# The projection of the per-layer input, moved from the first stage to the stretch before the last gate

## What is computed

```python
u = rms_norm(h, g_pre)
z = u @ w_in                       # 2048 x 22528, attention, retention, gates
...                                # attention, retention, merge of both
y = merged @ w_o
h = h + rms_norm(y, g_post)
h = h + sigmoid(h @ w_ple_gate) * (p @ w_ple_proj)
```

## Time and profile before

| | us |
|---|---|
| median of three runs | 3043.8 |
| the profiled execution | 3037.74 |
| its span | 3035.8 |
| PE busy | 2911.3 (96%) |
| DVE busy | 1772.7 (58%) |
| ACT busy | 1137.2 (37%) |
| granted PE clock over the span | 0.98 |

### The profile page before, as it was taken

One profiled execution on the slowest core, in us unless ns is written; L12 is line 12 of the kernel. 1 busy time (PEld: TensorE's weight loads), 2 busy tenths in 40 slices (PEclk: granted clock), 3 DMA queues, 4 the chain that ended last, 5 costly groups with the idle time before them and its releaser, 6 DMA issues.

```text
span 3035.8 us, 57013 instructions
## 1 busy us (share of the span) xinstructions
PE 2911.3 (96%) x23406; PEld 2856.8 (94%) x23406; DVE 1772.7 (58%) x3159; ACT 1137.2 (37%) x2078; POOL 362.2 (12%) x537
## 2 busy tenths in 40 slices
PE   6899999999999999999999999999999999997898
PEld 6899999999999998989999999999999999997897
DVE  5557666676566666576676676665654433424532
ACT  6344343444444433333333333434343222323222
POOL 2000000000001002112112112110001100001211
PEclk8999999999999999999999999999999999998899
DMA  8555656656566454456465456476657665554353
GB/s 254 160 168 176 205 170 201 193 184 193 168 190 194 161 194 158 140 192 210 153 212 188 157 199 215 158 256 213 246 198 290 214 234 191 205 187 147 116 186 110
DMA packets 380307, 575.64 MB, mean 190 GB/s; under 512 B 16456, under 2 KB 340872, under 8 KB 376840
## 3 DMA queue, kind: packets, MB, share of 16 engines
q1 hardware_dynamic: 336448, 428.32, 41.1%
q0 software_dynamic: 43600, 143.69, 15.6%
HBM read 515.67 MB, written 232.42 MB: 246 GB/s over the span
## 4 chain that ended last, share of the span: by engine, by line
PE 82%; DMA 5%; DVE 5%; DVEq 3%; ACT 2%; issue 1%; ACTq 1%; SPq 0%; POOL 0%; POOLq 0%
PE acc L524 52%; PE acc L536 21%; DMA raw_weights<-in_w_in 1%; PE aux L756 1%; PE aux L767 1%; DVEq L1704 1%; DVE weights L1287 1%; PE aux L777 1%; DVE stage_buffers L1873 1%; ACT weights L933 1%; DMA y_scr<-stage_buffers 1%; PE aux L649 1%; PE aux L833 1%; DVEq L1392 1%; DMA stage_buffers<-in_x_prompt 1%
## 5 line engine op out<-in xcount | busy, mean ns | idle before, releaser
L524 PE MATMUL acc<-moving,weights 128*128 128x260 f32 x12384 | 1574.5, 285 | 7.5 <-DVE sampled L1368 7.5
L524 PEld LDWEIGHTS acc<-moving,weights 128*128 128x128 f32 x12384 | 1516.8, 189 | 16.9 <-issue 8.3
L1287 DVE TENSOR_TENSOR weights<-raw_weights,weights 128x512 fp32r<-128x512 f32 (+1 forms) x1030 | 697.8, 686 | 707.5 <-ACT weights L933 660.0
L933 ACT ACTIVATE weights<-raw_weights 128x512 fp32r<-128x512 f32 (+1 forms) x1030 | 634.1, 625 | 1185.5 <-PE acc L524 438.7
L536 PE MATMUL acc<-moving,weights 128*128 128x260 f32 x5760 | 711.2, 286 | 48.8 <-DVE moving L1843 20.5
L536 PEld LDWEIGHTS acc<-moving,weights 128*128 128x128 f32 x5760 | 705.3, 191 | 52.2 <-DVE weights L1287 22.3
L524 PE MATMUL acc<-combined_moving,weights 128*128 128x260 f32 x3096 | 430.2, 289 | 3.2 <-DVE partial_sums L1401 2.4
L524 PEld LDWEIGHTS acc<-combined_moving,weights 128*128 128x128 f32 x3096 | 394.9, 191 | 8.9 <-issue 5.9
L1368 DVE SCALAR_TENSOR_TENSOR stage_buffers<-acc,partial_sums 128x260 f32<-128x260 f32 x344 | 146.5, 478 | 165.8 <-PE acc L524 165.7
L933 ACT ACTIVATE weights<-combined_weights 128x512 fp32r<-128x512 f32 x172 | 108.1, 629 | 295.8 <-PE acc L524 279.7
L1287 DVE TENSOR_TENSOR weights<-combined_weights,weights 128x512 fp32r<-128x512 f32 x172 | 118.5, 689 | 145.8 <-ACT weights L933 145.0
(11 more groups left out here) (256 smaller groups left out, 1783.8 us busy)
## 6 DMA issues: line engine op xcount, KB each, us to landing
out<-in_cache_win SPq DMA_DIRECT2D x128, 1023.5 KB, 8.8
raw_weights<-in_w_in SPq DMA_DIRECT2D x96, 1024.0 KB, 6.2
raw_weights<-in_w_in SPq DMA_DIRECT2D x160, 512.0 KB, 5.3
out<-in_cache_win SPq DMA_DIRECT2D x32, 1022.0 KB, 10.9
out<-stage_buffers POOLq DMA_DIRECT2D x120, 256.0 KB, 3.3
stage_buffers<-in_cache_win POOLq DMA_DIRECT2D x48, 512.0 KB, 5.5
stage_buffers<-in_state_ret POOLq DMA_DIRECT2D x64, 256.0 KB, 3.7
raw_weights<-in_w_r_out SPq DMA_DIRECT2D x16, 1024.0 KB, 7.3
```

The costliest lines, as they stand in the source:

```text
L524: mm = pe.matmul(acc[:, m, half, 0:HC], W[:, g % AHEAD, wp, kk, :], mov(up, kk), start=(start and kk == 0 and n == 0), stop=(stop and kk = ...
L933: act.activation(W[:, g % AHEAD, 0, 0:src.shape[1]], src, ACT.Copy).then_inc(s_whi, 1)
L1287: dve.tensor_tensor(W[:, g % AHEAD, 1, 0:src.shape[1]], src, W[:, g % AHEAD, 0, 0:src.shape[1]].bitcast(F32), ALU.subtract).then_inc(s_wre ...
```

## The change

The projection's 16 chunks are now a pair of their own, PL (mode P), between the w_o pairs and the gate pairs. p and its transposes move too: SP loads p at the first w_r pair, PE turns it within the third w_o pair. The split of p goes to a tile of its own (`turned`), and the 16 projected tiles stay on chip in memory that the seven-product pairs no longer use (`projected`). The DRAM scratch and its stores and loads are gone. In the first stage nothing but x is prepared; weights of pair 0 are loaded at once, and their first ten chunks are converted before or among the tiles of x. The first tiles prepared are now 8 to 15. In the stretch before the gate, ACT and DVE interleave the projection's conversions and copies with the tiles of h. For all pairs the half of `raw` whose chunk comes first is loaded first.

```diff
-       "F0": [("raw", c, m) for c in (1, 2, 3, 0) for m in range(2)],
-       "F1": [("raw", c, m) for c in (2, 3, 0, 1) for m in range(2)],
+       "F": [("raw", c, m) for c in (2, 3, 0, 1) for m in range(2)],
+       "P": [("two", n // 8, n % 8) for n in range(KD)],
...
     def halves_of(p):
-        return [half for half in (1, 0) if any(o[0] == "raw" and o[1] // 2 == half for o in OPS[p.mode])]
+        seen = [half_of(p.first + n) for n in range(p.n)]
+        return sorted({half for half in seen if half is not None}, key=seen.index)
...
-    FIRST_KS = [*range(4, KD), 2, 3, 0, 1]
+    FIRST_KS = [*range(8, KD), *range(8)]
...
+            if q == WR:
+                for slot in range(2):
+                    sp.wait_ge(s_rnewst[slot], 16 * QB * 2 * H)
+                sp.dma_start(p_nat, p_prompt[0, 0].rearrange("(t p) c -> p t c", p=P)).then_inc(s_xload[5], 16)
...
+            elif q == PL:
+                copies = 0
...
+        for q in range(WO, PL):
+            plain_pair(pairs[q], {0: [input_turns]} if q == WO + 2 else {}, ...)
+        pe.wait_ge(s_plo, 3)
+        for n in range(KD):
+            if n == 2:
+                square_means()
+            pe.wait_ge(s_wready, pairs[PL].first + n + 1)
+            acc_ready(n % 2)
+            ...  # 12 matmuls, as line 640 before
...
         for n in range(KD):
             act.wait_ge(s_u, count.due(s_u))
-            if n == KD - 2:
-                act.wait_ge(s_used, N_PLE)
             act.activation(U[:, 0, FIRST_KS[n], :], utmp[:, n % 4, :], ACT.Copy).then_inc(s_uhi, 1)
-            act.wait_ge(s_used, n + 1)
-            if n >= PPR:
-                act.wait_ge(s_ppst[n // 4 - 2], 16)
-            act.activation(halves(pp_out[:, n % PPR, :]), acc[:, n % 2, :, 0:HC], ACT.Copy).then_inc(...)
-            act.drain().then_inc(s_pp, 1)
-            hi(n + AHEAD)
+            if n in (9, 11, 13, 15):
+                hi(AHEAD + (n - 9) // 2)
...
+        for n in range(KD):
+            if n == 1:
+                norm_std()
+            projected_out(n)
+            hi(pairs[PL].first + n + AHEAD)
+            if n in (9, 11, 13, 15):
+                h_tile((n - 9) // 2)
+        for n in range(4, KD):
+            h_tile(n)
+            if n in (9, 11, 13, 15):
+                hi(pairs[WG].first + AHEAD + (n - 9) // 2)
...
+        g = pairs[PL].first + AHEAD
+        lo(g)
         dve.wait_ge(s_std, count.due(s_std))
         dve.reciprocal(nrs, nrs)
         dve.drain()
+        lo(g + 1)
         LAG = 3
         for n in range(KD + LAG):
             if n < KD:
+                normed_tile(n)
             if n >= LAG:
                 moving_lo(n - LAG, M)
+            if n < 7:
+                lo(g + 2 * n + 2)
+                lo(g + 2 * n + 3)
+            if n - LAG in (9, 11, 13, 15):
+                lo(pairs[WG].first + AHEAD + (n - LAG - 9) // 2)
```

More of the change, by code:

```diff
@@ L96 @@
 AHEAD = 6
-N_PLE = 16
 class Pair:
@@ L257, in build @@
     sg_in, tmp = t(2, TC), t(TC)
-    pp_in = t(2, TC)
+    p_rows = t(2 * TC)
+    p_nat, ps_nat = p_rows[:, 0:TB * PLE].rearrange("p (t c) -> p t c", t=TB), t(PLE)
+    pT = [turned[:, n] for n in range(2)]
+    projected = [*(projected_14[:, n, :] for n in range(14)), p_rows[:, 0:TC], p_rows[:, TC:2 * TC]]
     sqb, sqsum, nrs = sg_in, tmp, sg_in[:, 0, :]
@@ L888, in _, with input_turns @@
-        fills.add("norm", 0)
+        def input_turns():
+            pe.wait_ge(s_xload[5], count.due(s_xload[5], skip=1))
+            for j in range(2):
+                pe.wait_ge(s_free[2 + j], count.due(s_free[2 + j]))
+                for tb in range(TB):
+                    mm = pe.transpose(aux[:, 2 + j, tb * P:(tb + 1) * P], p_nat[:, tb, j * P:(j + 1) * P], ident[:])
+                mm.then_inc(s_full[2 + j], 1)
+                fills.add(f"p{j}", 2 + j)
+            pe.wait_ge(s_free[1], count.due(s_free[1]))
+            for j in range(2):
+                mm = pe.transpose(aux[:, 1, j * NS:(j + 1) * NS], ps_nat[0:NS, j * P:(j + 1) * P], ident[0:NS, 0:NS])
+            mm.then_inc(s_full[1], 1)
+            fills.add("ps", 1)
@@ new lines, in square_means @@
+        def square_means():
+            pe.wait_ge(s_sqsum, 1)
+            pe.wait_ge(s_free[0], count.due(s_free[0]))
+            pe.wait_ge(s_free[1], count.due(s_free[1]))
+            pe.matmul(aux[:, 0, 0:HC], mean_d[:], sqsum[:, 0:HC], start=True, stop=True)
+            pe.matmul(aux[:, 1, 0:HC], mean_d[:], sqsum[:, HC:TC], start=True, stop=True).then_inc(s_full[0], 1)
+            fills.add("norm", 0)
+        for q in range(WO, PL):
+            plain_pair(pairs[q], {0: [input_turns]} if q == WO + 2 else {},
+                       {n: 2 * KD + H + n + 1 for n in range(KD)} if q == WO else None)
@@ new lines, in _ @@
+        pe.wait_ge(s_plo, 3)
[4 more added lines that the diff above has]
+            acc_ready(n % 2)
+            for k in range(2):
+                for m, (wp, up) in enumerate(passes):
+                    for half, (a, b) in enumerate(halfcols):
+                        mm = pe.matmul(acc[:, n % 2, half, 0:HC], W[:, (pairs[PL].first + n) % AHEAD, wp, k, :],
+                                       pT[up][:, k, a:b], start=(k == 0 and m == 0), stop=(k == 1 and m == 2))
+            mm.then_inc(s_used, 1)
@@ new lines, in projected_out, with norm_std @@
+        def projected_out(n):
+            act.wait_ge(s_used, pairs[PL].first + n + 1)
+            act.activation(halves(projected[n]), acc[:, n % 2, :, 0:HC], ACT.Copy).then_inc(s_accfree[n % 2], 1)
+        def norm_std():
+            act.wait_ge(s_sqsum, 1)
+            act.activation(nrs[:, 0:1], eps, ACT.Sqrt)
+            act.drain()
+            act.wait_ge(s_full[0], filled.due("norm"))
+            act.activation(nrs[:, 0:HC], aux[:, 0, 0:HC], ACT.Sqrt, bias=eps[:, 0:1]).then_inc(s_free[0], 1)
+            act.activation(nrs[:, HC:TC], aux[:, 1, 0:HC], ACT.Sqrt, bias=eps[:, 0:1]).then_inc(s_free[1], 1)
+            act.drain().then_inc(s_std, 1)
@@ new lines, in h_tile @@
+        def h_tile(n):
+            act.wait_ge(s_h, n + 1)
+            act.activation(U[:, 0, n, :], M[:, n, :], ACT.Copy).then_inc(s_uhi, 1)
+        for i in range(KD // 2):
+            mine = {3: [lambda: output_tile(i, 0)], 7: [lambda: output_tile(i, 1)]}
+            if i == 2:
+                mine[1] = [turned_input]
+            steps(pairs[WO + i], mine)
+        for n in range(KD):
+            if n == 1:
[4 more added lines that the diff above has]
+                h_tile((n - 9) // 2)
@@ L1566, in _ @@
             for j in range(5):
-                steps(pairs[ATT + 5 * h + j], tiles[j], hooks[j])
+                steps(pairs[ATT + 5 * h + j], tiles[j], hooks[j], split=0 if h or j else 4)
         def new_buffers():
```

187 lines of the change are left out of this document (73 added, 114 removed).

## The result

The changed kernel takes 3003.8 us (median of 4 runs, 3002.6 to 3004.4); beside it on the same chip the kernel before took 3042.9 (median of 4). The ratio is 0.987, 95% interval 0.9853 to 0.9888. The profiled execution took 3004.39 us, its span is 3002.6.

The account below looks back on a forecast made before the run. PE's matmuls bound the kernel, so gains come only where PE stands still; VectorE's chain bounds the first stage. First stage -30.5, turning p +1.1, stretch before the gate -0.5 make -29.9 us: 3014 us, range 3008 to 3024.

Parts of the forecast that it names:

- PE does not wait for weights there, so nothing: Plain pairs: loading the first needed half of the weights earlier gains nothing, since PE does not wait for weights.
- Start of normalising: 33.1 stays ... even.: First stage: VectorE still starts normalising x at 33.1 us, dropped differences of p balancing wider conversions (+1.6 us).
- 16 x 0.67 + 16 x 0.61 + 4 x 0.61 = 22.9: First stage: VectorE's scalings, low parts and conversions take 22.9 us, so combining can start at 56.0 instead of 86.53.
- The rival of transfers: First stage bound by transfers: weights or tables come 6 us late, gain 24.5, total 3020 us; chance 10%.
- The stretch before the gate, "-0.5": End of w_o to the gate's second pair: 0.5 us shorter, between -4 and +7.
- The gate's other pairs ... nothing.: Later gate pairs lose 14 fetches of projected tiles, but PE runs gapless there, so no gain.
- The median lies 6.1 above it.: Whole kernel: the median of runs lies 6.1 us above the profiled execution, turning 3007.8 into 3013.9.
- the tiles progressed under the projection: Answers a rival before the gate: tiles of h don't progress under the projection, total 3021 us; chance 12%.
- the change did what it says: Answers the no-effect case in the first stage: combining doesn't move up, about 3043 us; chance 3%.
- the clock held: Answers the slower case: PE's clock falls to 0.50 in projection and first gate pair, 3052 us; chance 4%.
- Better than forecast: Before the gate: PE keeps its clock, first gate pair ends 2.9 + 1.8 - 0.5 earlier, 3010 us; chance 9%.
- -30.5 for the first stage: First stage: PE restarts after pair 0 at 75.05 instead of 105.58, 30.5 us earlier.

Follow-up runs that it names:

- b_newhalf: The kernel before with the change's load order of the `raw` halves alone; 3030.1 us, ratio 0.9962.
- b_again: The kernel before, unchanged, timed and profiled a second time; 3040.7 us, ratio 1.0000.
- b_late: The kernel before with the combining of blocks moved behind the eviction of pair 0, into pair 1; 3035.3 us, ratio 0.9978.
- a_noprod: The changed kernel with ten of the twelve matmuls of each projected tile left out; 3000.7 us, ratio 0.9874.
- a_again: The changed kernel, unchanged, timed and profiled a second time; 3001.2 us, ratio 0.9878.
- a_late: The changed kernel with the combining of blocks moved behind the eviction of pair 0, into pair 1; 2992.7 us, ratio 0.9844.

## Why the prediction was wrong

The direction, the place of the gain and its main term were right. The sum of about 30 had to be 39 by the medians, 37 of it steady in the traces. Of the 7 us between, the load order of the weights, which I had put at nothing, can account for the most. By its steps:

- **"PE does not wait for weights there, so nothing" (the order of the halves).** This step failed. PE did wait, 1.56 and 1.74 us at the first pairs of w_r and w_o; the list of waits has them beneath VectorE's lines, and I took them for the norms and merges that are evicted there. b_newhalf shows that they are the load order's: without them, w_a, w_r and w_o take 3.5 us less than in b_again. With the turn of p, +1.1 as forecast (2618.94 to 2620.12 in the trace after), -0.9 to -2.1 came for my +1.1. On the kernel before, the order by itself also takes 2 to 4 us off the stretch before the gate, as much as the change did, and 6 to 7.5 us off the first stage.
- **"Start of normalising: 33.1 stays ... even."** The scaling starts 2.0 us earlier in the first pair of traces, 0.1 later in the unchanged ones and 0.6 earlier without copies. 0.5 of it is the change: counted from the turn of the last block of x, at the same clock, it comes after 13.45 us before (b_late) and 12.93 after. The differences of p stood ahead of the sums over features, on which the scaling waits; I had counted VectorE's work and not that order. The rest is when x landed and the clock of that turn, below.
- **"16 x 0.67 + 16 x 0.61 + 4 x 0.61 = 22.9", tables, restart.** Right: 31.08 to 54.17 is 23.1; the tables were asked for at 46.3 and not waited for; from combining to restart 19.05, as forecast; restart at 73.2 for 75.05, by the earlier start alone. The rival of transfers falls.
- **The stretch before the gate, "-0.5".** Measured -2.2 to -3.7, inside the bounds given. The reason given for the first half of it failed: tile 7 is not held by the projection's end on PE (a_noprod), but by two conversions a tile on VectorE. It came at Z + 31.2, 2 us later than forecast. The conversions among the last tiles cost 1.05 each on balance, for 0.6. At the seam to the gate's second pair the errors had cancelled, by luck: Z + 60.4, for Z + 62.0 less 1.5. What I left out lies behind it: the 48 matmuls up to the first turn took 7.6 us before, at a clock of 0.77 after the wait for the sigmoid, and 6.0 after, at 1.00 without that wait.
- **"The gate's other pairs ... nothing."** 1.3 us came at the very end, between the last store's issue (3027.10 before, 2995.19 after) and the end of the span (8.7 and 7.4 us), alike in all three pairs of traces. No run tells why.
- **"The median lies 6.1 above it."** This step held. The profiled execution was a quick one (3037.74, where 17 runs beside a_again had a median of 3039.9), and the gain between the medians is the larger one. Without the 6.1 I'd have said 3007.8, nearer to 3003.8, but only because a base too low and a gain too small cancel: the steady 37 us make 3005.9 from the median of 3042.9, and 3000.7 from the profiled execution. What remains of the 39 beyond the 37 is the stage that wanders, where I can't say which wait it is.

The rivals: the tiles progressed under the projection; the first stage wasn't bound by transfers; the change did what it says; and the clock held. *Better than forecast* was nearest in time (3010, given 9%), though two of its three terms were others than those that came. That -30.5 for the first stage came almost exactly is in part luck too: the traces scatter over 2 us there by the landing of x and the clock.

## What to carry to other kernels

When a change also reorders loads, count the short waits at each seam between stages, however they are labelled, and ask for each which transfer came last: here the load order alone took 10 us off the kernel before, and without it the changed kernel is 18 to 25 us slower. Where two engines alternate, an instruction put between costs more than its own time there, but judge it by what it releases: the early conversions paid for themselves through an earlier load. Take a gain from several traces, stage by stage, and set it against the median and not against the one profiled execution: that one may have been quick.

## What was not expected of the hardware

- The turn of the last block of x (16 transposes of 128x128) took 3.68 us or 1.97, in either kernel: 3.68 in the traces of before, b_again and a_again, 1.97 in after, b_late and a_late, and once 2.15 (b_newhalf). The granted clock over it was 0.50 (1.2 GHz) in before and 1.00 (2.4 GHz) in after; in the five us ahead of it PE had turned one block in either. It moved the start of the scaling by 0.5 us: from the turn's start to the scaling 13.91 before and in b_again, 13.45 in b_late; 13.39 in a_again, 12.93 after. The turn itself starts anywhere from 18.2 to 19.2, when x has landed. Window of before, and of after (columns as above):

```profile
19.20:22.80 3.60, 3.60 (x17) 3.27 (x17) 0.69 (x1) 3.17 (x5) 0.00 (x0) 0.50 1.18 300
```

```profile
18.20:20.10 1.90, 1.90 (x16) 1.67 (x16) 0.69 (x1) 1.90 (x3) 0.00 (x0) 1.00 1.20 291
```

- Copies of cache rows that nothing on chip waits for cost 21 us of 3040, and moving 24 of 168 of them to another stage gave some 6 back.
